# Attention in eight steps: two score tiles are issued beside logit tiles, and a step's last turned tiles and its values are moved behind the logits of later steps

## The reference, cut to what matters

```python
def _stick_breaking_attention(q, k, v):          # 8 heads, per block of 128 queries
    z = jnp.einsum('bqhd,bkhd->bhqk', q_blk, k) * scale
    log_keep = jnp.where(causal, jax.nn.log_sigmoid(-z), 0.0)
    later = lax.cumsum(log_keep, axis=3, reverse=True) - log_keep
    log_w = jnp.where(causal, jax.nn.log_sigmoid(z) + later, -jnp.inf)
    return jnp.einsum('bhqk,bkhd->bqhd', jnp.exp(log_w), v)

def _dilated_branch(q, k, v, rel_bias, window, dil):   # 8 heads, three windows, merged by softmax weights
    s = jnp.einsum('nbqhd,nbkhd->nbhqk', qb, kb) / math.sqrt(dh) + bias
    p = jnp.exp(s - jnp.max(s, axis=-1)[..., None])
    l = jnp.sum(p, axis=-1)
    num = jnp.einsum('nbhqk,nbkhd->nbqhd', p, vb)
```

## Time and profile before

| | |
|---|---|
| median of 3 runs | 2593.22 us (2593.08 to 2597.55) |
| the profiled execution: its own time | 2594.58 us |
| its span | 2592.8 us |
| TensorE busy | 2491.6 us, 96% |
| ScalarE busy | 984.8 us, 38% |
| VectorE busy | 1040.2 us, 40% |
| GpSimd busy | 1294.6 us, 50% |
| mean granted clock of TensorE | 0.987 |

### The profile page before, as it was taken

One profiled execution on the slowest core, in us unless ns is written; L12 is line 12 of the kernel. 1 busy time (PEld: TensorE's weight loads), 2 busy tenths in 40 slices (PEclk: granted clock), 3 DMA queues, 4 the chain that ended last, 5 costly groups with the idle time before them and its releaser, 6 DMA issues.

```text
span 2592.8 us, 31087 instructions
## 1 busy us (share of the span) xinstructions
PE 2491.6 (96%) x11446; PEld 2012.7 (78%) x11446; DVE 1040.2 (40%) x1488; ACT 984.8 (38%) x1325; POOL 1294.6 (50%) x681
## 2 busy tenths in 40 slices
PE   8999999999899999999999999998999998998997
PEld 6888887856788888888888778687888887877676
DVE  3222322145722212322241650545222692724885
ACT  5333333366433333433333333434333433233553
POOL 5555455400465554655544544236555554246873
PEclk9999999999999999999999999999999999999999
DMA  4333442200233333233333223012333444333751
GB/s 139 96 97 97 146 129 90 89 17 1 65 106 97 97 98 108 87 97 95 94 104 104 75 87 98 17 49 82 97 97 97 146 154 163 107 90 88 185 133 65
DMA packets 79995, 251.68 MB, mean 97 GB/s; under 512 B 9731, under 2 KB 14211, under 8 KB 79788
## 3 DMA queue, kind: packets, MB, share of 16 engines
q1 hardware_dynamic: 72384, 235.55, 30.0%
q10 hardware_dynamic: 6684, 11.90, 1.5%
q0 software_dynamic: 848, 3.15, 0.4%
HBM read 237.54 MB, written 15.25 MB: 97 GB/s over the span
## 4 chain that ended last, share of the span: by engine, by line
PE 70%; issue 10%; DVE 8%; POOL 7%; DMA 3%; ACT 3%; SPq 0%; POOLq 0%; DVEq 0%; ACTq 0%
PE banks L1837 19%; PE banks L1838 18%; PE banks L1839 18%; POOL wl_sb L385 5%; DMA raw_sb<-weights 2%; PE banks L1903 2%; PE banks L1904 2%; PE banks L1909 2%; DVE mix_sb L2204 1%; POOL xl_sb L416 1%; PE banks L1783 1%; PE banks L657 1%; PE banks L1790 1%; PE banks L885 1%; PE banks L894 1%
## 5 line engine op out<-in xcount | busy, mean ns | idle before, releaser
L385 POOL TENSOR_TENSOR wl_sb<-raw_sb,wh_sb 128x1024 fp32r<-128x1024 f32 x401 | 974.0, 2431 | 976.4 <-ACT wh_sb L377 973.6
L1837 PE MATMUL banks<-xh_sb,wh_sb 128*128 128x512 f32 x2016 | 790.0, 392 | 17.0 <-POOL wl_sb L385 17.0
L1838 PE MATMUL banks<-xh_sb,wl_sb 128*128 128x512 f32 x2016 | 786.1, 390 | 0.0
L1839 PE MATMUL banks<-xl_sb,wh_sb 128*128 128x512 f32 x2016 | 785.8, 390 | 0.0
L377 ACT ACTIVATE wh_sb<-raw_sb 128x1024 fp32r<-128x1024 f32 x401 | 424.9, 1060 | 781.2 <-DMA raw_sb<-weights 767.7
L1837 PEld LDWEIGHTS banks<-xh_sb,wh_sb 128*128 128x128 f32 x2016 | 379.2, 188 | 108.0 <-POOL wl_sb L385 15.3
L1839 PEld LDWEIGHTS banks<-xl_sb,wh_sb 128*128 128x128 f32 x2016 | 379.1, 188 | 79.2
L1838 PEld LDWEIGHTS banks<-xh_sb,wl_sb 128*128 128x128 f32 x2016 | 379.3, 188 | 77.9 <-issue 0.2
L1837 PE MATMUL banks<-hh_sb,wh_sb 128*128 128x512 f32 x704 | 274.1, 389 | 0.2 <-POOL wl_sb L385 0.2
L1838 PE MATMUL banks<-hh_sb,wl_sb 128*128 128x512 f32 x704 | 274.0, 389 | 0.0
L1839 PE MATMUL banks<-hl_sb,wh_sb 128*128 128x512 f32 x704 | 274.0, 389 | 0.0
(11 more groups left out here) (368 smaller groups left out, 2693.9 us busy)
## 6 DMA issues: line engine op xcount, KB each, us to landing
raw_sb<-weights SPq DMA_DIRECT2D x404, 512.0 KB, 3.6
park<-xs_sb ACTq DMA_DIRECT2D x12, 512.0 KB, 3.6
mix_sb<-scratch SPq DMA_DIRECT2D x16, 258.0 KB, 5.7
hf_sb<-scratch SPq DMA_DIRECT2D x16, 258.0 KB, 5.1
mix_sb<-park SPq DMA_DIRECT2D x4, 1024.0 KB, 7.1
scratch<-scratch ACTq DMA_DIRECT2D x1, 2560.0 KB, 12.1
scratch<-mix_sb SPq DMA_DIRECT2D x8, 259.5 KB, 2.9
x_sb<-x_in SPq DMA_DIRECT2D x8, 256.0 KB, 8.5
```

The lines of the kernel that those rows point to most:

```text
L385: pool.tensor_tensor(wl[:, slot, :], raw[:, slot, :], wh_f[:, slot, :], ALU.subtract).then_inc(w_split, 1)
L1837: pe.matmul(dst, wh[:, q, cols], in_hi, start=first, stop=False)
L1838: pe.matmul(dst, wl[:, q, cols], in_hi, start=False, stop=False)
L1839: return pe.matmul(dst, wh[:, q, cols], in_lo, start=False, stop=last)
```

## The change

TensorE, from step 1 on: score 3 is issued between logits 2 and 3, and score 2 right behind logit 0. Turns 1, 2 and 3 of step u-1 follow the logits of step u, and the values of step u-2 follow these. ScalarE: score exponential 0 stands between the two halves of `soften`; the copies of turns 1 to 3 of step u-1 stand behind score exponential 2 of step u. VectorE: the bias of score 3 is added early, and biases and maxima are separate steps. Score rows (`ssb`) and turned tiles (`pT`) have two buffers, the exponentials (`ab`) one.

```diff
-        ab = [region(22016 + PACKED * e, PACKED) for e in range(2)]
-        pT = chunks(region(16384, 4 * T))
-        ssb = [hf_f[:, T * j:T * (j + 1)] for j in range(4)]
+        pT = [chunks(region(16384 + 4 * T * e, 4 * T)) for e in range(2)]
+        ab = region(23040, PACKED)
+        ssb = [[hf_f[:, T * j:T * (j + 1)] for j in range(4)],
+               [hf_f[:, 2944:3072], hf_f[:, 3328:3584], hf_f[:, 2560:2944], hf_f[:, 2048:2560]]]
...
+        def taken(u):
+            return (0, 1, 3, 2) if u else (0, 1, 2, 3)
+        def nth(u, j):
+            return 4 * u + taken(u).index(j) + 1
...
@@ logits_and_scores
                 logit(u, 2)
+                if u:
+                    score(u, 3)
                 logit(u, 3)
...
                 logit(u, 0)
+                score(u, 2)
                 hide_later((0,))
-                score(u, 2)
-                if u:
-                    score(u, 3)
...
@@ turn
                 if j >= 2:
                     pe.wait_ge(a_tc, 4 * u + j - 1)
                 elif j == 1:
-                    pe.wait_ge(a_sadd, 4 * u + 4)
+                    pe.wait_ge(a_sadd, nth(u + 1, 3) if u + 1 < UNITS else 4 * u + 4)
+                    if u + 1 == UNITS:
+                        pe.wait_ge(a_tc, 4 * u)
...
@@ attention_tensor, the loop
-                if u:
-                    both_values(u - 1)
+                if 1 <= u <= UNITS:
+                    for j in (1, 2, 3):
+                        turn(u - 1, j)
+                if u >= 2:
+                    both_values(u - 2)
                 if u < UNITS:
                     suffix_sums(u, (1, 2, 3))
                     turn(u, 0)
                     suffix_sums(u, (0,))
-                    for j in (1, 2, 3):
-                        turn(u, j)
...
@@ attention_scalar
-            def soften(u):
-                if u > 1:
-                    act.wait_ge(a_rc, 2 * (u - 1))
+            def soften(u, part):
+                if u:
+                    act.wait_ge(a_rc, 2 * u)
...
-                if u:
-                    copy_turned(u - 1, 2)
-                    copy_turned(u - 1, 3)
                 if u < UNITS:
-                    soften(u)
+                    soften(u, 1)
                     exps(u, 0)
+                    soften(u, 0)
                     logs(u)
                     exps(u, 1)
-                if u and u % 2 == 0:
-                    high_of(a_osb, 6, u // 2 - 1)
-                    high_of(a_odl, 7, u // 2 - 1)
-                if u < UNITS:
                     exps(u, 2)
...
+                if 1 <= u <= UNITS:
+                    for j in (1, 2, 3):
+                        copy_turned(u - 1, j)
+                if u >= 3 and u % 2:
+                    high_of(a_osb, 6, (u - 3) // 2)
+                    high_of(a_odl, 7, (u - 3) // 2)
+                if u < UNITS:
                     weights_of(u, 1)
                     copy_turned(u, 0)
                     exps(u, 3)
                     weights_of(u, 0)
-                    copy_turned(u, 1)
...
@@ attention_vector, the loop
                     add_bias(u, 0)
                     add_bias(u, 1)
+                    row_maximum(u, 0)
+                    row_maximum(u, 1)
+                    if u:
+                        add_bias(u, 3)
                     least(u, 1)
+                    if u:
+                        row_maximum(u, 3)
                     least(u, 0)
```

More of the change, by code:

```diff
@@ L626, in score @@
                     pe.wait_ge(a_sadd, 4 * u + 2)
-                elif j == 3 and u:
-                    pe.wait_ge(a_tc, 4 * u)
+                elif j == 3 and u > 1:
+                    pe.wait_ge(a_tc, 4 * u - 4)
                 qb = ROWS[j]
@@ L656, in suffix_sums @@
                     dst = zcols(kb)
-                    last = pe.matmul(dst, negtri, packed(sp_[u % 2], kb), start=False, stop=(kb == 3),
+                    last = pe.matmul(dst, negtri, packed(sp_, kb), start=False, stop=(kb == 3),
                                      skip_group_check=True)
@@ L660, in suffix_sums @@
                         last = pe.matmul(dst[:, P * (later - kb):T - P * kb], negones[:, :],
-                                         packed(sp_[u % 2], later), start=False, stop=True, skip_group_check=True)
+                                         packed(sp_, later), start=False, stop=True, skip_group_check=True)
                 last.then_inc(a_rc, 1)
@@ L673, in turn @@
                 for kb in range(qb + 1):
-                    last = pe.transpose(banks[:, TURN_BANK[j], P * kb:P * (kb + 1)], ssb[qb][:, P * kb:P * (kb + 1)],
-                                        ident)
+                    last = pe.transpose(banks[:, TURN_BANK[j], P * kb:P * (kb + 1)],
+                                        ssb[u % 2][qb][:, P * kb:P * (kb + 1)], ident)
                 last.then_inc(a_t, 1)
@@ L687, in both_values @@
                     d = other(u)
-                    its = pe.matmul(banks[head(d), 7, P * kb:T], vd[:, kb, 64 * d:64 * d + 64], pT[:, kb, P * kb:T],
+                    its = pe.matmul(banks[head(d), 7, P * kb:T], vd[:, kb, 64 * d:64 * d + 64], pT[u % 2][:, kb, P * kb:T],
                                     start=(kb == 0), stop=(kb == 3), skip_group_check=True)
@@ L693, in attention_tensor @@
             value_tiles(0)
-            for u in range(UNITS + 1):
+            for u in range(UNITS + 2):
                 if u < UNITS:
@@ L706, in attention_tensor @@
                     suffix_sums(u, (0,))
-                    for j in (1, 2, 3):
-                        turn(u, j)
         def attention_scalar(act):
-            def soften(u):
-                if u > 1:
-                    act.wait_ge(a_rc, 2 * (u - 1))
-                for part in (1, 0):
-                    act.wait_ge(a_z, 2 * u + 2 - part)
-                    act.activation(two(ab[u % 2])[part], Z23 if part else Z01, ACT.Exp).then_inc(a_ex, 1)
+            def soften(u, part):
+                if u:
+                    act.wait_ge(a_rc, 2 * u)
+                act.wait_ge(a_z, 2 * u + 2 - part)
+                act.activation(two(ab)[part], Z23 if part else Z01, ACT.Exp).then_inc(a_ex, 1)
             def logs(u):
@@ L720, in logs @@
                     act.wait_ge(a_abs, 2 * u + 2 - part)
-                    buf = two(ab[u % 2])[part]
+                    buf = two(ab)[part]
                     act.activation(buf, buf, ACT.Ln, bias=1.0).then_inc(a_ln, 1)
@@ L776, in spare_sum @@
                 dve.wait_ge(a_ln, 2 * u + 2 - part)
-                buf = two(sp_[u % 2])[part]
+                buf = two(sp_)[part]
                 dve.tensor_tensor(buf, Z23 if part else Z01, buf, ALU.max).then_inc(a_spr, 1)
@@ L821, in attention_vector @@
                     normalise(u, 0)
-                    add_bias(u, 3)
-                    for j in (1, 2, 3):
+                    if u == 0:
+                        add_bias(u, 3)
+                        row_maximum(u, 3)
+                    for j in (1, 2):
                         normalise(u, j)
-                if u and u % 2 == 0:
-                    low_of(a_oev, 6, u // 2 - 1, u - 1)
-                    low_of(a_oev2, 7, u // 2 - 1, u)
+                if u >= 3 and u % 2:
+                    low_of(a_oev, 6, (u - 3) // 2, u - 2)
+                    low_of(a_oev2, 7, (u - 3) // 2, u - 1)
+                if u < UNITS:
+                    normalise(u, 3)
         c_row, m_row, e_row = (region(16384 + T * j, T)[0:HEADS, :] for j in range(3))
```

34 lines of the change are left out of this document (20 added, 14 removed).

## The result

| | before | after |
|---|---|---|
| median | 2595.39 us (4 runs, 2593.08 to 2599.09) | 2634.52 us (4 runs, 2631.7 to 2637.79) |
| the profiled execution: time, span | 2594.58, 2592.8 us | 2636.75, 2635.0 us |
| first logit to the first matmul of the output projection | 138.6 us | 174.0 us |
| mean granted clock | 0.987 | 0.976 |

The ratio is 1.015, with a 95% interval from 1.0129 to 1.017: slower by 1.5%, as forecast (2633 us).

The account below looks back on a forecast made before the run. TensorE was taken to bound the steady step (15.17 of 16 us busy). +22.0 us at full clock and +17.5 us for the slow clock gave +39.5 on a median of 2593.2: 2633 us, range 2612 to 2646.

Parts of the forecast that it names:

- The copy wait: TensorE before turn 3, steps 1 to 7: idle some 5.7 us for ScalarE's copy of turn 1, against 0.40 before.
- S+9.8: Forecast start of turn 3, 9.8 us after S, the first logit matmul of a step.
- The walk along ScalarE: ScalarE's instructions added up from a step's first logit: copy of turn 1 at 9.3 us, turn 3 0.5 later.
- The sum at full clock: Attention steps: period 17.15 us against 13.79, step 1 14.8, net +22.0 us.
- The slow clock: Each of seven waits lowers TensorE's clock, half the slow stretch lost: 2.5 us a step, 17.5 us; chance 0.77.
- The sign "19 to 20.5 us in steps 2 to 7": Period that would show the forecast right, 2.3 us less in step 1.
- bounds of 1.7 and 3.2: Range of us lost a step to the lower clock, half of a slow stretch; 2.5 taken as the middle.
- The gains: Step 1 starts 2.5 us earlier: moved turns 1.67, score 2 beside logit 0 0.85.
- The tail: TensorE after the last suffix sums: turns 1 to 3, values of units 6 and 7, 6.3 us.
- The clock did not stay up: Rival: same wait in each period, but TensorE stays at 2.4 GHz, +22 us, 2615; chance 0.10.
- The scores do share time with the logits: Opposed rival: score 3 serialises with the logits, 0.72 us a step, 2638; chance 0.07 together with slow for longer.
- The case "copy early": Rival: copy of turn 1 doesn't hold turn 3, period 11.75 us, -13.4 us, 2580; chance 0.04.

Follow-up runs that it names:

- wait filled: Changed kernel plus six pairs of thrown-away 512-column matmuls ahead of turn 3 in steps 1 to 7: 2612.93 us, ratio to before 1.0044 to 1.0082.
- copy early: Changed kernel with ScalarE's copy of turned tile 1 right behind the second exponential, ahead of logarithms and table loads: 2584.31 us, in a second comparison 2588.1 us.
- turn 0 last: Changed kernel with turn 3 behind the values, tile 1 copied between the logarithms, turn 0 behind the last suffix sum and its copy behind the last weights: 2585.88 us.
- scores alone: Kernel before with only score 3 beside logits 2 and 3 and score 2 beside logit 0: 2594.18 us, ratio 0.9986 to 1.0005.

## Why the prediction was right

**The copy wait.** Forecast: 5.7 us, turn 3 at S+9.8. Measured: 5.72 us, S+9.77, in all seven steps. The walk along ScalarE held to 0.1 us in each entry, and moving the copy or turn 3 takes the loss away.

**The sum at full clock.** Forecast period 17.15 us; with the wait filled it is 17.16. Step 1 without values was forecast at 14.8, and was 14.66 with the wait filled and 17.03 with the slow clock.

**The slow clock.** Forecast 2.5 us a step, 17.5 in all. The seven periods end 133.0 us after step 1 begins (533.72 to 666.72); without the slow clock they are 14.8 + 6 x 17.15 = 117.7. So it cost 15.3 us, 2.2 a step. It differs by step: the periods from step 2 on are 19.52, 19.95, 18.57, 19.51, 19.95 and, up to turns 1 to 3 behind step 7, 18.47. The sign "19 to 20.5 us in steps 2 to 7" thus held in four of six. The trace shows why they differ. The clock is low for 6.8 us in every step, but it falls at another place of the wait each time, and the part that lies in the wait costs nothing. In the step of 18.57 us TensorE works 3.07 us of the slow stretch; in the one before it, of 19.95 us, 5.85:

```profile
579.07:585.89 6.82, 5.85 (x20) 2.72 (x21) 1.05 (x4) 2.28 (x6) 0.00 (x0) 0.50 0.01 2
```

Half of these, 1.5 and 2.9 us, are what the two periods are above 17.16 (1.4 and 2.8). The prediction's bounds of 1.7 and 3.2 came from stretches in which TensorE worked nearly throughout; its middle of 2.5 was a choice, and that it came near is partly luck.

**The gains.** Step 1 began 34.9 us after the first logit in place of 39.1: 4.2 us where 2.5 were forecast. Most of the 1.7 us more is step 0's own slow clock: 3.4 us of slow work (528.0 to 531.4) in place of 6.45; half of the difference is 1.5. The tail was 6.13 us, forecast 6.3.

```profile
666.72 0.82 PE L683 MATMUL banks<-consts_sb,hf_sb 128*128 128x128 f32 x6
667.94 0.52 PE L683 MATMUL banks<-consts_sb,hf_sb 128*128 128x128 f32 x3 [0.40 <-ACT mix_sb L752]
...
672.85 0.50 PE L1929 MATMUL banks<-xh_sb,wh_sb 128*128 128x512 f32 x1
```

The sum of these for the stretch is -4.2 + 133.0 + 6.1 - 99.5 = +35.4 us, where the prediction had +39.5. The medians differ by 39.1. That the time came out closer than its parts is chance: 0.8 us of the profiled difference of 42.2 lie ahead of attention and 6.0 behind it, about 4.5 of these in the mLSTM section, where the kernels don't differ. There a slow stretch lasted 17.1 us in the changed kernel and 6.8 before:

```profile
1668.00:1685.10 17.10, 17.10 (x27) 7.58 (x26) 8.89 (x16) 3.56 (x3) 2.05 (x8) 0.50 0.00 0
1685.10:1692.00 6.90, 6.90 (x43) 5.33 (x41) 2.36 (x5) 2.13 (x3) 0.00 (x0) 1.00 0.00 0
```

```profile
1629.10:1635.90 6.80, 5.76 (x8) 2.56 (x9) 1.93 (x4) 1.27 (x1) 0.90 (x1) 0.50 0.14 57
1635.90:1643.00 7.10, 6.42 (x19) 3.16 (x19) 5.14 (x9) 1.27 (x1) 1.15 (x5) 1.00 0.00 0
```

**What bounded the kernel before.** The prediction took TensorE as the bound of the steady step. With 1.69 us of its work gone the period stayed at 13.80, so the chain over ScalarE and VectorE bounded it just as much; the 0.21 us wait was the sign. The sum did not suffer, because behind turn 3 TensorE's queue alone sets the pace, and the suffix sums of the changed kernel show no wait for VectorE.

**The rivals.** The clock did not stay up. The copy did hold. The scores do share time with the logits: score 3 added nothing that moved the first exponential (S+2.15 against S+2.14). The case "copy early" was priced at a period of 11.75 us; the real one is 12.65 until the wait for turned tile 2 goes too, and 11.9 to 12.2 then. That case would have come out faster, but by some 6 to 10 us of time rather than 13.

The rule of the Trainium skill (TensorE: Matmul & The Clock Gate, "HAM oscillation — how this bites in real kernels") says that a loop whose every turn makes TensorE wait starts each burst of matmuls at the lower clock, and that half of the slow time is lost. The trace agrees: a fall in each of the seven waits of 5.72 us, half of the slow work lost, and with the waits filled no fall.

Not tried: the second buffers without the later values, or the later values undone. Whether the new order needs them is open.

## What to carry to other kernels

When a step of an in-order queue is moved, list what each of its waits is for and where the releasing instruction stands on the other engine's queue, and then what stands behind it on its own. A 0.4 us wait at the end of a step became 5.7 us with the whole ring behind it. Moving the 0.38 us copy forward on ScalarE took it away, and so did moving turn 3 back on TensorE with the copy left late. Work taken off a busy engine gained nothing here, because a chain through other engines set the restart; the short wait at that restart was the sign of it.

## What was not expected

- The same code had slow stretches of different length from run to run: 6.8 and 17.1 us in the mLSTM section, with TensorE busy throughout the longer one. This may be part of why kernels here are hard to tell apart below 3 us (not shown beyond these two profiles): the repeats of one kernel lie 2 to 11 us apart.
- Every kernel waits the same 2.51 us in step 0. The granted clock fell behind that wait in six of the nine profiles and stayed at 1.00 in three (copy early, wait filled, turn 0 last), which is worth some 3.2 us at most. A wait of 1.91 us in seven steps (scores alone) has a low clock behind it once, from 627.5 to 630.9. The single wait of 2.54 to 3.21 us in step 1 of the five kernels with the copy or turn 3 moved brought it down in all five, and the 5.72 us wait each time.
- Matmuls whose results are thrown away, put into the wait, made the changed kernel 0.9% faster.
